# Retention and grouped attention: strips built a head ahead, rotations beside head 0, the last norm inside the attention's first steps

## The reference

```python
# per head and direction, lg = log(1 - exp(rate))
intra  = where(rel >= 0, exp(lg * rel), 0)         # decay by distance
scores = (q @ k.T) * intra                          # q, k rotated
o      = scores @ v + (q @ state) * exp(lg * (idx + 1))
state  = sum over the 256 context tokens of (k * decay) v   # forward and backward
# then, per head and token
o = (o - mean(o)) * rsqrt(var(o) + eps) * gn_g * silu(gate)
```

## Time and profile before

| | us |
|---|---|
| median of 3 runs | 1925.18 |
| lowest, highest run | 1919.43, 1929.16 |
| profiled execution, in all | 1921.84 |
| its span in the profile | 1920.0 |
| PE, DVE, ACT, POOL busy in the span | 1752.0, 1038.2, 703.3, 101.8 |

### The profile page before, as it was taken

The page is one execution under the profiler, slowest core; times in us unless marked ns, Lnnn a source line. Parts: engine busy times, 40 slices in busy tenths (PEclk is TensorE's granted clock), DMA queues, the critical chain, the costliest instruction groups (busy, mean ns, idle before and its releaser), DMA issues. The chain is left out here.

```text
span 1920.0 us, 36446 instructions
## 1 busy us (share of the span) xinstructions
PE 1752.0 (91%) x16002; PEld 1357.3 (71%) x16002; DVE 1038.2 (54%) x1481; ACT 703.3 (37%) x1059; POOL 101.8 (5%) x125
## 2 busy tenths in 40 slices
PE   7999688888888999999999989997889889999997
PEld 5666566676766778888888768883347768888885
DVE  6666454554533666767675674225678354443433
ACT  4444434232312544323232544224556244232322
POOL 2000000000000010000011110001010100000001
PEclk9999898989888999999999999999889989999998
DMA  5112220101004434444664131222000212333231
GB/s 196 66 55 77 85 78 26 36 20 36 31 15 165 144 111 153 143 165 163 210 219 168 55 107 56 68 97 74 1 1 1 88 66 99 99 99 99 88 99 55
DMA packets 49182, 173.47 MB, mean 90 GB/s; under 512 B 5552, under 2 KB 6960, under 8 KB 48128
## 3 DMA queue, kind: packets, MB, share of 16 engines
q1 hardware_dynamic: 39184, 134.62, 20.5%
q0 software_dynamic: 9840, 36.51, 5.7%
HBM read 162.46 MB, written 8.65 MB: 89 GB/s over the span
## 5 line engine op out<-in xcount | busy, mean ns | idle before, releaser
L363 PE MATMUL pair<-h_hi,w_hi 128*128 128x512 f32 x1032 | 416.5, 404 | 33.8 <-DVE w_lo L401 15.6
L364 PE MATMUL pair<-h_lo,w_hi 128*128 128x512 f32 x1032 | 404.9, 392 | 0.0
L365 PE MATMUL pair<-h_hi,w_lo 128*128 128x512 f32 x1032 | 404.5, 392 | 0.0
L401 DVE TENSOR_TENSOR w_lo<-w_raw,w_hi 128x1024 fp32r<-128x1024 f32 (+2 forms) x225 | 266.0, 1184 | 214.2 <-ACT w_hi L386 214.1
L386 ACT CAST w_hi<-w_raw 128x1024 fp32r<-128x1024 f32 (+2 forms) x225 | 221.8, 989 | 223.7 <-PE pair L365 219.6
L363 PEld LDWEIGHTS pair<-h_hi,w_hi 128*128 128x128 f32 x1032 | 195.5, 189 | 93.0 <-DVE w_lo L401 32.3
L364 PEld LDWEIGHTS pair<-h_lo,w_hi 128*128 128x128 f32 x1032 | 195.6, 190 | 42.2 <-issue 3.8
L365 PEld LDWEIGHTS pair<-h_hi,w_lo 128*128 128x128 f32 x1032 | 195.5, 189 | 42.0
L363 PE MATMUL pair<-ff_f_hi,w_hi 128*128 128x512 f32 x512 | 199.7, 390 | 0.5 <-DVE w_lo L401 0.5
L364 PE MATMUL pair<-ff_f_lo,w_hi 128*128 128x512 f32 x512 | 199.2, 389 | 0.0
L365 PE MATMUL pair<-ff_f_hi,w_lo 128*128 128x512 f32 x512 | 199.2, 389 | 0.0
(11 more groups left out here) (433 smaller groups left out, 2541.0 us busy)
## 6 DMA issues: line engine op xcount, KB each, us to landing
w_raw<-in_w_ff SPq DMA_DIRECT2D x128, 512.0 KB, 3.3
mod_w<-in_w_mod POOLq DMA_DIRECT2D x48, 512.0 KB, 3.6
w_raw<-in_w_in SPq DMA_DIRECT2D x22, 512.0 KB, 3.3
w_raw<-in_w_gate SPq DMA_DIRECT2D x16, 512.0 KB, 3.4
w_raw<-in_w_out SPq DMA_DIRECT2D x16, 512.0 KB, 3.3
w_raw<-in_w_rwkv SPq DMA_DIRECT2D x15, 512.0 KB, 3.3
w_raw<-in_w_da SPq DMA_DIRECT2D x12, 512.0 KB, 3.9
g_spill<-norm_pair POOLq DMA_DIRECT2D x16, 256.0 KB, 3.1
```

The source lines that it names most:

```text
L363: nc.tensor.matmul(out, w_hi, x_hi, start=(k == 0), stop=False)
L364: nc.tensor.matmul(out, w_hi, x_lo, start=False, stop=False)
L365: last = nc.tensor.matmul(out, w_lo, x_hi, start=False, stop=(k == kt - 1))
L401: nc.vector.tensor_tensor(lo[:, s % SPLIT_SLOTS, 0:cols], pr.raw[:, w % RAW_SLOTS, 0:cols], hi[:, s % SPLIT_SLOTS, 0:cols].bitcast(F32), A ...
```

## The change

- The 8 rotations take the order query 0, key 0, query 1, key 1 and so on (`TURN`). Two stand in the front part, behind the transposes; PE issues four between head 0's scores and its output, two behind the output. The cosine product goes from DVE to POOL.
- POOL squares the grouped attention's tiles behind these eight products.
- The strip of head h+1 is made at the end of head h: ACT makes its exponentials behind the norm's factor, POOL multiplies both by `rel` (in head 0 still DVE), DVE adds. The context keys are decayed there too, ahead of the strip. Both stand in DVE's list ahead of the centring of the last output.
- The Silus go from the front to head 0 of ACT's list.
- The fifth pass goes. Mean, centring and square of head 3 stand in step 0 of the grouped attention, variance, log and factor in step 1, norm and gate in step 2, high part in step 3, low part in step 4 (`last_head`).
- Rotations of the grouped attention move: the first to head 2, the second and third to head 3, the last two to step 0, their sums to steps 1 to 3. Some banks change.

```diff
-        self.normed_in = {(2, 0): (0, 1), (3, 0): (2, 3), (4, 0): (4, 5)}
-        self.turned_in = {(2, 1): (0,), (3, 1): (1, 2), (4, 1): (3, 4)}
+        self.normed_in = {(1, 1): (0, 1), (2, 1): (2, 3), (3, 1): (4, 5)}
+        self.turned_in = {(2, 0): (0,), (3, 0): (1,), (3, 1): (2,)}
 
     def turn_bank(self, j):
-        return self.pr.bank[(3, 3, 5, 5, 7)[j]]
+        return self.pr.bank[(7, 7, 4, 5, 6)[j]]
 
...
+    def pool_squares(self, pool):
+        for n, (x, w) in enumerate(self.items):
+            self.pr.nc.gpsimd.tensor_tensor(self.sq[n][:, :], x, x, ALU.mult).then_inc(self.s["sq"], 1)
+
+    def pool(self, pool, h):
+
         nc, s = self.pr.nc, self.s
-        for n, (x, w) in enumerate(self.items):
-            nc.gpsimd.tensor_tensor(self.sq[n][:, :], x, x, ALU.mult).then_inc(s["sq"], 1)
-        pool.wait_ge(s["in"], 32)
-        for j, n in enumerate(self.turned):
-            x = self.items[n][0]
+        if h == 2:
+            pool.wait_ge(s["in"], 32)
+        for j in {2: (0,), 3: (1, 2, 3, 4)}.get(h, ()):
+            x = self.items[self.turned[j]][0]
             pool.wait_ge(s["rot"], j + 1)
             nc.gpsimd.tensor_tensor(x, x, self.table[:, 0, :], ALU.mult).then_inc(s["cos"], 1)
 
-    def pe(self, pe, h, point):
...
-                grouped.pool(pool)
+                pool.wait_ge(s["rope_in"], 32)
+                for i, v in enumerate(TURN):
+                    pool.wait_ge(s["rot"], i + 1)
+                    nc.gpsimd.tensor_tensor(V[:, v, :], V[:, v, :], table[:, 0, :], ALU.mult).then_inc(s["cos"], 1)
+                grouped.pool_squares(pool)
+                pool.wait_ge(s["in"], 48)
+                for h in range(1, H):
+                    pool.wait_ge(s["e1"], 2 * h + 2)
+                    pool.wait_ge(s["strip"], 3 * h)
+                    pool.wait_ge(s["sout"], TB * h)
+                    nc.gpsimd.tensor_tensor(strip[:, 0, :], strip[:, 1, :], rel[:, 2, :], ALU.mult).then_inc(s["strip"], 1)
+                    nc.gpsimd.tensor_tensor(strip_b[:, :], strip_b[:, :], rel[:, 3, :], ALU.mult).then_inc(s["strip"], 1)
+                    grouped.pool(pool, h)
...
+                pe.wait_ge(s["rope_in"], 32)
+
+                def turn(i):
+                    if i >= 6:
+                        pe.wait_ge(s["sin"], i - 3)
+                    nc.tensor.matmul(turn_bank(i), rot_sb[:, :], V[:, TURN[i], :], start=True, stop=True).then_inc(s["rot"], 1)
+
+                for i in range(2):
+                    turn(i)
                 pe.wait_ge(s["trout"], 8)
...
+                def last_head(n):
+                    if n == 0:
+                        mean(H - 1)
+                    if n == 1:
+                        variance(H - 1)
+                    if n == 2:
+                        pe.wait_ge(s["log"], H)
...
+                        variance(h - 1)
+                    else:
+                        for i in range(2, 6):
+                            turn(i)
+                    grouped.pe(pe, h, 0, (s["stateout"], 2 * h + 2), (s["centred"], h))
...
+                    if h == 0:
+                        for i in range(6, 8):
+                            turn(i)
+                        pe.wait_ge(s["sin"], 8)
+                    grouped.pe(pe, h, 1, (s["stateout"], 2 * h + 2), (s["centred"], h))
+                grouped.pe_steps(pe, last_head, (s["oout"], H))
...
+                def decays(h):
+                    for d in range(2):
+                        if h:
+                            act.wait_ge(s["strip"], 3 * h)
+                        nc.scalar.activation(strip[:, 1, :] if d == 0 else strip_b[:, :], rel[:, d, :], ACT.Exp,
+                                             scale=sm[:, 5, 4 * d + h:4 * d + h + 1]).then_inc(s["e1"], 1)
...
+                def last_head(n):
+                    if n == 0:
+                        square(H - 1)
+                    if n == 1:
+                        log(H - 1)
+                        factor(H - 1)
+                    if n == 3:
+                        high_part(H - 1)
+
+                decays(0)
+                for h in range(H):
...
-                            act.wait_ge(s["lo"], h - 1)
-                        nc.scalar.copy(o[:, h % 2, :], pr.bank[2]).then_inc(s["oout"], 1)
+                    if h + 1 < H:
+                        decays(h + 1)
+                    if h == 0:
+                        for i in range(H):
+                            nc.scalar.activation(V[:, 12 + i, :], V[:, 12 + i, :], ACT.Silu).then_inc(s["silu"], 1)
...
+                def turned_tile(i):
+                    v = V[:, TURN[i], :]
                     dve.wait_ge(s["rot"], i + 1)
                     if i >= 2:
                         dve.wait_ge(s["roped"], i - 1)
-                    nc.vector.tensor_tensor(turned[:, i % 2, :], pr.bank[i % 2], table[:, 1, :], ALU.mult).then_inc(s["sin"], 1)
-                    nc.vector.tensor_tensor(V[:, i, :], V[:, i, :], table[:, 0, :], ALU.mult).then_inc(s["cos"], 1)
+                    nc.vector.tensor_tensor(turned[:, i % 2, :], turn_bank(i), table[:, 1, :], ALU.mult).then_inc(s["sin"], 1)
                     dve.wait_ge(s["sin"], i + 1)
                     dve.wait_ge(s["cos"], i + 1)
-                    nc.vector.tensor_tensor(V[:, i, :], V[:, i, :], turned[:, i % 2, :], ALU.add).then_inc(s["roped"], 1)
-                dve.wait_ge(s["roped"], 8)
...
+                def make_strip(h):
+                    if h == 0:
+                        dve.wait_ge(s["e1"], 2)
                         dve.wait_ge(s["in"], 48)
-                        if h:
-                            dve.wait_ge(s["strip"], 3 * h)
-                            dve.wait_ge(s["sout"], TB * h)
                         nc.vector.tensor_tensor(strip[:, 0, :], strip[:, 1, :], rel[:, 2, :], ALU.mult).then_inc(s["strip"], 1)
...
+                keys(0)
+                make_strip(0)
+                for h in range(H):
+                    j = h - 1
+                    if h:
+                        centre(j)
+                    dve.wait_ge(s["strip"], 3 * h + 3)
...
+                    if h == 0:
+                        for i in range(2, 8):
+                            turned_tile(i)
                     grouped.dve(dve, h, 0)
                     if h:
-                        dve.wait_ge(s["rstd"], j + 1)
-                        nc.vector.scalar_tensor_tensor(x, x, pr.param("gn_g")(j), rstd[:, j % 2, :], ALU.mult, ALU.mult)\
-                            .then_inc(s["y"], 1)
-                        dve.wait_ge(s["y"], 2 * j + 1)
-                        dve.wait_ge(s["silu"], j + 1)
-                        nc.vector.tensor_tensor(x, x, V[:, 12 + j, :], ALU.mult).then_inc(s["y"], 1)
-                        dve.wait_ge(s["hi"], j + 1)
-                        nc.vector.tensor_tensor(out_lo[:, j, :], x, out_hi[:, j, :].bitcast(F32), ALU.subtract).then_inc(s["lo"], 1)
+                        result(j)
+                    if h + 1 < H:
+                        keys(h + 1)
+                        make_strip(h + 1)
+                    if h:
+                        low_part(j)
                     grouped.dve(dve, h, 1)
-                grouped.dve_steps(dve)
+                grouped.dve_steps(dve, last_head)
...
+                if 1 <= n <= 3:
+                    self.dve_added(dve, (n + 1,))
```

More of the change, by code:

```diff
@@ L1635, in pe_steps @@
                             last.then_inc(s["score"], 1)
+            last_head(n)
+            if n == 0:
+                for j in (3, 4):
+                    self.pe_turn(pe, j)
             if n >= 2:
@@ new lines, in square, with log, factor @@
+                def square(j):
+                    act.wait_ge(s["centred"], j + 1)
+                    nc.scalar.activation(sq[:, j % 2, :], o[:, j % 2, :], ACT.Square).then_inc(s["sq"], 1)
+                def log(j):
+                    act.wait_ge(s["var"], j + 1)
+                    nc.scalar.activation(rstd[:, j % 2, :], pr.bank[6 if j < H - 1 else 7], ACT.Ln, scale=1.0 / P, bias=pr.eps(0))\
+                        .then_inc(s["log"], 1)
+                def factor(j):
+                    act.wait_ge(s["log"], j + 1)
+                    nc.scalar.activation(rstd[:, j % 2, :], rstd[:, j % 2, :], ACT.Exp, scale=-0.5).then_inc(s["rstd"], 1)
@@ new lines, in high_part @@
+                def high_part(j):
+                    act.wait_ge(s["y"], 2 * j + 2)
+                    nc.scalar.copy(out_hi[:, j, :], o[:, j % 2, :]).then_inc(s["hi"], 1)
+                def last_head(n):
+                    if n == 0:
+                        square(H - 1)
[6 more added lines that the diff above has]
+                for h in range(H):
+                    j = h - 1
+                    for d in range(2):
+                        if h:
+                            act.wait_ge(s["o"], h)
+                        nc.scalar.activation(dq[:, d, :], steps[:, d, :], ACT.Exp,
```

(25 more changed lines are left out.)

179 lines of the change are left out of this document (91 added, 88 removed).

## The result

The changed kernel takes 1934.62 us, the median of 7 runs (1929.41 to 1937.44), against 1925.18 before (1919.43 to 1929.82, 7 runs beside them). The ratio is 1.0046 with a 95% interval of 1.0025 to 1.0067: slower by 9 us, of which the interval leaves 5 to 13. I had forecast slower by 7.2.

What follows compares the result with a forecast made beforehand. No engine is full in the block: PE, ACT and DVE hand over in a ring, and its last instruction counts. -1.1 + 12.4 + 1.6 + 0.3 - 9.3 + 3.3 = +7.2 us gave 1932.4 for the median, range 1920 to 1938.

Steps and rivals of the forecast that it cites:

- front: Block start to head 0's first score product: fewer rotations ahead, ACT's copies behind a DMA; -1.1 us, between -3.0 and +0.8.
- head 0 to 1: Between first score products: POOL's cosines, six squares and strip products delay head 1; +12.4 us, the term that decides.
- head 1 to 2: Between first score products: exponentials, POOL's strip products, then DVE's sum and centring come last; +1.6 us.
- head 2 to 3: Between first score products: same chain as a head earlier, with PE at full clock sooner; +0.3 us.
- head 3 to first maximum: Head 3's first score product to the grouped attention's first maximum: the loop's fifth pass goes; -9.3 us.
- steps: Grouped attention's steps: head 3's norm, with two table loads, adds work; +3.3 us, bounds 1.5 to 5.
- Rival (c): At the heads: POOL is not last, so heads start earlier; -11.7 us, 1913.5; chance 0.10.
- rival (b): As (a), plus one more half-clock stretch on PE and DVE locked once more; +11 us, 1936; chance 0.22.
- (a): The forecast itself: POOL sets the start of each head; 1926 to 1935 us, likeliest 1932.4; chance 0.54.
- The sum stays: Head 1's key decays could wait for POOL's squares, up to 4 us on DVE, without changing the forecast sum.

Runs made afterwards that it cites:

- e2: The changed kernel with ACT's exponentials for the next strip moved ahead of the norm's square, log and factor; 1.0001 of the time before.
- e4: The changed kernel with the strip's two products back on DVE for heads 1 to 3, still made at the end of the head before; ratio 0.9999.
- e3: The changed kernel with POOL's six squares back at the block's start and ACT's next-strip exponentials ahead of the norm's square; ratio 0.9967 to the kernel before.
- e6: The changed kernel with early strip exponentials, squares first and all eight rotations ahead of the transposes; ratio 0.9900 to the kernel before.
- e7: e3 with head 3's log and factor replaced by copies, so no table loads in attention step 1; ratio 0.9959 to the kernel before.
- e9: The changed kernel with the five pieces of head 3's norm ahead of the attention's step 0; ratio 1.0090 to the kernel before.
- e1: The changed kernel with POOL's six squares put back at the block's start, nothing else; ratio 1.0029 to the kernel before.
- e10: e6 with the strip's products on DVE, and keys and strip ahead of the norm's result; ratio 0.9900 to the kernel before.

## Why the prediction was right, step by step

| term | forecast | measured in the traces |
|---|---|---|
| front | -1.1 | -1.0 |
| head 0 to 1 | +12.4 | +12.7 |
| head 1 to 2 | +1.6 | +1.2 |
| head 2 to 3 | +0.3 | +1.2 |
| head 3 to first maximum | -9.3 | -8.3 |
| steps | +3.3 | +3.0 |
| sum | +7.2 | +8.8 |

The mechanism held: POOL was last ahead of each head. The largest term hit closely because two small misses in it cancel: the six squares took 6.5 us, not 5.8, and the two products 4.1, not 4.4. The terms of the front add up to 1333.3 (1329.1 + 0.9 + 3.3), not to the 1333.1 that the forecast has, so by them it is -0.9. A product of 128x896 took 2.08 us where I took 2.22, inside my bounds of 1.82 and 2.57, and e2 and e4 take that wait away or shorten it from two sides and gain 8 us each, of which 1.7 behind head 3 came by the clock. Rival (c) needed a price of 1.02. A head as short as it wanted appeared only once POOL's work was started early (e3: 13.7 us for head 1, though 17.6 for head 2), and the block of e3 is 5.0 us under before's. Its sum of -11.7 was passed only where the rotations, which it left beside head 0, went forward too (e6, -19.1).

Mis-sized were three terms. "Head 2 to 3, +0.3" measured +1.2 and "head 3 to the grouped attention, -9.3" measured -8.3: I had counted PE there at full clock, but behind the waits for POOL it ran at the half one. The windows view of after for the third scores and variance behind each first product:

```profile
1361.00:1365.00 4.00, 3.89 (x5) 1.70 (x6) 1.55 (x4) 1.40 (x2) 0.00 (x0) 0.57 0.00 0
1382.00:1386.00 4.00, 4.00 (x7) 1.71 (x6) 2.17 (x4) 0.82 (x2) 0.00 (x0) 0.63 0.00 0
1403.00:1406.00 3.00, 3.00 (x6) 1.20 (x5) 1.89 (x3) 0.69 (x1) 0.00 (x0) 0.59 0.00 0
```

So stretches at half clock, rival (b)'s ground, did come in heads 2 and 3, beside (a). They were not more than the kernel before had there (granted 0.87 and 0.89, against 0.92 and 0.90 in after), and PE had idled 3.2 us ahead of head 1's third score, not the 7 of rival (b). What was wrong was leaving them out of the sum: behind head 3 the stretch takes 15.3 us at full clock (e2, e4) and 17.0 in after, on either side of my 16.0. In e6, where PE no longer waits that long, the granted clock is 1.00 in heads 0 and 1 together (26.85 us), and in head 2:

```profile
1354.05:1371.65 17.60, 15.32 (x40) 6.32 (x38) 14.54 (x19) 10.96 (x17) 5.79 (x3) 1.00 0.00 1
```

"The steps, +3.3" was right in size (+3.0) and partly wrong in cause: I charged 2.0 us to the two table loads with the log and the factor, and without the loads (e7) only 1.25 came back. The whole norm costs 2.2 in that step (7.02 against e9's 4.83); the rest stands in DVE's list, which has no gap there in e7. The drain of 1.38 us that the Trainium skill adds to each switch ("ScalarE: Activation LUTs", What ACT_TABLE_LOAD costs) shows in no row. ACT's timeline of after, in attention step 1:

```profile
1426.43 1.28 ACT L1910 ACT_TABLE_LOAD   x1
1427.72 0.69 ACT L1910 ACTIVATE rt_turned<-pair,consts 128x512 f32<-128x512 f32 x1
1428.43 1.28 ACT L1915 ACT_TABLE_LOAD   x1
1429.72 0.63 ACT L1915 ACTIVATE rt_turned<-rt_turned 128x512 f32<-128x512 f32 x1
```

Each operation starts 0.01 us behind its load.

"The sum stays" on the keys was right, too, but with less room than I had thought: DVE's wait behind them was 5.0 us, not some 7. The rule of the Trainium skill ("SBUF — State Buffer", Who interferes with whom) that tensor_scalar can block and be blocked at the shared port is borne out on its losing side by 3.62 us beside POOL's squares against 0.87. That tensor_scalar also holds POOL up shows in no row: the four squares beside it took 4.02 us against 4.0 alone. In e1, where the strip was no longer late, the keys took over as the bound.

## What to carry to other kernels

Work moved beside other work is hidden only if the engine that takes it is done before the next hand-over, and every list that it is put ahead of must be followed to its end: here six squares moved behind the rotations delayed the strip's products behind them in POOL's list, and the late strip the centring behind it in DVE's. Before moving work out of a front part, look at what the front waits for: here a DMA held it for 12 us, and all eight rotations there left it as long as with two (28.5 against 28.7 us). And when work is built a step ahead, start its first operation a step ahead as well; the change moved the strip's products forward but left their exponentials behind the norm.

## What was not expected

A stall of POOL and DVE on each other appears in no wait of the profile; it is only a longer operation (2.56 us for one of 0.75, 3.62 for four that take 0.87), so a group's mean has to be compared with its minimum. And POOL's help with the strips was not needed once the order was right: DVE alone (e10, with keys and strip a little earlier in its list) was no slower, with a block 3.4 us shorter.

The entry into the block differed by up to 14 us between profiled executions of kernels with the same code ahead of it, half as much again as the whole effect of the change. Only the block's own length could be read from a single trace.
